# A state-space layer by chunks of four steps, with its matrices made during the feed-forward part ahead of it, and the pool half first

## The reference, cut to what matters

```
first block, for each of 2 layers:
    x = layer_norm(ALPHA*x + 0.5*swiglu(x, ffn1)); x = layer_norm(ALPHA*x + hybrid attention(x))
    x = layer_norm(ALPHA*x + 0.5*swiglu(x, ffn2))        # 1024 -> 2*2816 -> 1024
second block, layer 0:
    h = x @ ab_w_in                                      # 1024 -> 512 (state space) + 512 (pool)
    mix = concat(s5_mixer(h[:, :512]), pool_mixer(h[:, 512:])) @ ab_w_out
    x = layer_norm(ALPHA*x + mix)
    x = layer_norm(ALPHA*x + mixture of 16 experts(x) + gated projection of p)
layer 1: the same with stick-breaking attention as the mixer
```

## Time and profile before

| what | us |
|---|---|
| median of 3 runs | 1889.21 (1889.15 to 1889.84) |
| the profiled execution's own time | 1889.26 |
| its span | 1887.5 |
| last feed-forward part, about | 825 to 1009 |
| `s5_and_pool` on PE, about | 1009.5 to 1179.1 |
| PE busy over the span | 1787.5 (95%) |
| DVE, ACT, POOL busy | 953.6, 611.0, 149.4 |

### The profile page before, as it was taken

How to read it: one execution, slowest core, us unless ns; L and a number is a source line. 1 busy time by engine, 2 the same in 40 slices (tenths; PEclk the granted TensorE clock), 3 DMA queues, 4 the chain that set the end, 5 groups by cost and what they waited for, 6 DMA issues and landing times.

```text
span 1887.5 us, 24150 instructions
## 1 busy us (share of the span) xinstructions
PE 1787.5 (95%) x9722; PEld 1327.3 (70%) x9722; DVE 953.6 (51%) x1313; ACT 611.0 (32%) x750; POOL 149.4 (8%) x123
## 2 busy tenths in 40 slices
PE   6999999999999999999999678999998999999996
PEld 5888878788878888777887336855554777755553
DVE  3654767555555556768546994511113666511113
ACT  3543443443344335436434212210002344110110
POOL 1000051000000004110000340000000000000000
PEclk9999999999999999999999788999999999999998
DMA  7555532555455545064555002799998433799993
GB/s 274 186 179 198 195 118 90 200 188 191 178 201 184 194 178 201 24 239 179 190 188 185 21 0 89 286 422 421 421 422 322 162 134 123 313 421 421 422 422 127
DMA packets 59710, 420.43 MB, mean 223 GB/s; under 512 B 6737, under 2 KB 6737, under 8 KB 10225
## 3 DMA queue, kind: packets, MB, share of 16 engines
q1 hardware_dynamic: 55728, 404.78, 55.4%
q0 software_dynamic: 3904, 14.55, 2.3%
HBM read 418.25 MB, written 1.05 MB: 222 GB/s over the span
## 4 chain that ended last, share of the span: by engine, by line
PE 84%; DVE 9%; ACT 3%; issue 2%; POOL 1%; DMA 1%; DVEq 0%; POOLq 0%; ACTq 0%
PE hh L1089 12%; PE y L569 10%; PE y L571 10%; PE y L570 10%; PE hh L569 8%; PE hh L571 8%; PE hh L570 8%; PE turn L1115 6%; PE y L1128 3%; PE turn L1013 3%; ACT w_hi L1243 1%; DVE w_lo L1631 1%; DVE work L2054 1%; PE turn L685 1%; DVE work L2063 1%
## 5 line engine op out<-in xcount | busy, mean ns | idle before, releaser
L1631 DVE TENSOR_TENSOR w_lo<-raw,w_hi 128x2048 fp32r<-128x2048 f32 x181 | 410.9, 2289 | 159.2 <-ACT w_hi L1243 159.1
L1243 ACT ACTIVATE w_hi<-raw 128x2048 fp32r<-128x2048 f32 x193 | 364.6, 1912 | 64.9 <-DMA raw<-units 64.9
L569 PE MATMUL hh<-w_hi,xt_hi 128*128 128x512 f32 x704 | 279.8, 397 | 1.8 <-DVE xt_lo L1736 1.8
L571 PE MATMUL hh<-w_hi,xt_lo 128*128 128x512 f32 x704 | 275.3, 391 | 0.0
L570 PE MATMUL hh<-w_lo,xt_hi 128*128 128x512 f32 x704 | 275.2, 391 | 0.0
L569 PE MATMUL y<-w_hi,xt_hi 128*128 128x512 f32 (+1 forms) x480 | 191.7, 399 | 7.0 <-DVE xt_lo L2080 2.8
L571 PE MATMUL y<-w_hi,xt_lo 128*128 128x512 f32 (+1 forms) x480 | 186.9, 389 | 0.0
L570 PE MATMUL y<-w_lo,xt_hi 128*128 128x512 f32 (+1 forms) x480 | 186.9, 389 | 0.0
L569 PEld LDWEIGHTS hh<-w_hi,xt_hi 128*128 128x128 f32 x704 | 132.9, 189 | 30.1 <-DVE xt_lo L1736 2.9
L571 PEld LDWEIGHTS hh<-w_hi,xt_lo 128*128 128x128 f32 x704 | 132.7, 188 | 28.4
L570 PEld LDWEIGHTS hh<-w_lo,xt_hi 128*128 128x128 f32 x704 | 132.9, 189 | 26.3
(11 more groups left out here) (298 smaller groups left out, 2144.1 us busy)
## 6 DMA issues: line engine op xcount, KB each, us to landing
raw<-units SPq DMA_DIRECT2D x289, 1024.0 KB, 10.6
late<-units SPq DMA_DIRECT2D x96, 1024.0 KB, 11.3
ln_gb<-ln_g POOLq DMA_DIRECT2D x6, 512.0 KB, 4.0
ln_gb<-ln_b POOLq DMA_DIRECT2D x6, 512.0 KB, 5.6
x_rows<-x POOLq DMA_DIRECT2D x2, 512.0 KB, 10.0
work<-window_matrices POOLq DMA_DIRECT2D x1, 1024.0 KB, 11.0
ln_gb<-ln_mix_g POOLq DMA_DIRECT2D x2, 512.0 KB, 4.4
ln_gb<-ln_mix_b POOLq DMA_DIRECT2D x2, 512.0 KB, 5.3
```

What stands on the lines that cost most here:

```text
L569: pe.matmul(dst, left[0], right[0], start=start, stop=False)
L571: return pe.matmul(dst, left[1], right[0], start=False, stop=stop)
L1243: act.activation(hi[r][:, :], raw[r][:, :], ACT.Copy).then_inc(hi_ready, 1)
L1631: dve.tensor_tensor(lo[r][:, :], raw[r][:, :], hi[r][:, :].bitcast(F32), ALU.subtract)\
```

## The change

The recurrence is taken in chunks of four time steps. B' is multiplied by `lam^0` to `lam^3` (`in_weights`), so that one matmul of 64 columns (K = 4 steps x 32 inputs) gives what a chunk adds to the state; the scan runs over 64 chunks with `|lam|^4`; C is multiplied by `lam^1` to `lam^4` (`out_weights`), so that the state at a chunk's start gives four outputs; what the inputs of a chunk do to its own outputs goes through a 128x128 matrix for each distance 0 to 3 (`k_mat`). Four tiles of states are one scan of 256 columns, so there are 4 scans for each part, not 16. POOL has no part in it: DVE turns back as well.

The matrices, and the sines (now 128x1024 in all), are made during the last feed-forward part: DVE has seven asides instead of two, ACT three and then copies, PE three small pieces in each of four steps. For this the loop of that part is written out. The pool half of `x @ ab_w_in` comes first; the state-space half comes transposed from PE and is spread by ACT into `u_p` and `u_s` (one copy of 256 columns and 16 of 32x64 for each quarter). The window means use 144, 16 and 112 columns. Three quarters of the pool half's output product fill places between the `outputs`. `decay` lies where `h` and `gate_act` do. POOL clears two buffers with memsets, takes three small loads for five, and loads `p` only after the last scan.

```diff
--- before.py
+++ after.py
@@ POOL, last feed-forward part, and ahead of load_p(0)
+                    pool.memset(work[:, 3072:8192], 0.0).then_inc(zeros_made, 1)
+                    pool.memset(work[:, 10240:13312], 0.0).then_inc(zeros_made, 1)
...
+            pool.wait_ge(st_ready, 4)
             load_p(0)
-            for i in range(S5_TILES):
...
-                for j in range(2):
-                    pool.tensor_tensor(n5[b][:, j], s5[:, b], trig[i // 4 % 2][:, j, q:q + 1, :].broadcast_to([P, 2, T]),
@@ PE, feed-forward part: a step, written out up to step 9
                 def step(j):
+                    if beside is not None:
+                        beside(j, 0)
                     tile(h_bank, half=first_half)
+                    if beside is not None:
+                        beside(j, 1)
                     down(j == 1, False)
+                    if beside is not None:
+                        beside(j, 2)
                     turn_h()
@@ PE, s5_and_pool
+                def states(c):
+                    pe.wait_ge(u_ready, c + 1)
...
+                    for q in range(4):
+                        for ri in range(2):
+                            at = (4 * ri + q) * N_CHUNKS
+                            mm = pe.matmul(h_bank[c % 2][:, at:at + N_CHUNKS], w_in[:, c, ri, q, :], u_s[:, c, q, :],
+                                           start=True, stop=True)
+                def outputs(c):
+                    if c >= 2:
+                        pe.wait_ge(y_read, c - 1)
+                    dst = turn_bank[c % 2]
+                    for d in range(CHUNK):
+                        pe.matmul(dst[:, d * N_CHUNKS:T], k_mat[:, c, d, :],
...
+                    pe.wait_ge(st_ready, c + 1)
+                    for j in range(CHUNK):
+                        for ri in range(2):
+                            for q in range(4):
+                                mm = pe.matmul(dst[32 * q:32 * q + 32, j * N_CHUNKS + 1:(j + 1) * N_CHUNKS],
...
+                features(0)
+                features(1)
+                states(0)
+                features(2)
+                states(1)
+                features(3)
+                window_means()
+                states(2)
+                outputs(0)
+                pool_mix()
+                states(3)
+                outputs(1)
+                pe.wait_ge(xt_lo_ready, seen(xt_lo_ready))
+                pool_part(0, 0)
+                outputs(2)
+                pool_part(0, 1)
+                outputs(3)
+                pool_part(1, 0).then_inc(unit_used, 1)
+                pe.wait_ge(bu_read, 4)
                 w = unit(4)
...
+                gate(w, 0, 4)
+                pool_part(1, 1).then_inc(unit_used, 2)
+
                 pe.wait_ge(xt_lo_ready, seen(xt_lo_ready, 2))
...
+                four(y_bank[1][0][:, :], w[0], 0, 1, first=False, last=True).then_inc(unit_used, 1)
+                turn_x(0)
+                four(y_bank[1][1][:, :], w[1], 0, 1, first=False, last=True).then_inc(unit_used, 1)
@@ ACT, s5_and_pool
+                def features(m):
+                    act.wait_ge(u_done, m + 1)
...
+                    act.activation(u_p[:, m], src, ACT.Copy)
+                    for q in range(4):
+                        for k in range(CHUNK):
+                            ins = act.activation(u_s[32 * k:32 * k + 32, m, q, :], src[32 * q:32 * q + 32, CHUNK - 1 - k, :],
+                                                 ACT.Copy)
@@ DVE, asides of the last feed-forward part
+                return (s5_parameters, lambda: (s5_angles(), out_weights(1)), lambda: (out_weights(2), out_weights(3)),
+                        lambda: (out_weights(4), in_weights(0))) + tuple(lambda c=c: in_weights(c) for c in range(1, 4))
@@ DVE, s5_and_pool
+                    dve.tensor_tensor(m5[:, 0], bu, both(trig[:, 0]), ALU.mult).then_inc(dve_link, 1)
+                    dve.tensor_tensor(m5[:, 1], bu, both(trig[:, 1]), ALU.mult).then_inc(bu_read, 1)
...
+                    dve.tensor_tensor(m5[:, 0, 0], m5[:, 0, 0], m5[:, 1, 1], ALU.add).then_inc(dve_link, 1)
+                    dve.tensor_tensor(m5[:, 0, 1], m5[:, 0, 1], m5[:, 1, 0], ALU.subtract).then_inc(dve_link, 1)
...
+                        dve.tensor_tensor_scan(m5[:, 0, ri], wide(decay), m5[:, 0, ri], 0.0, ALU.mult, ALU.add)\
...
+                    link(dve.tensor_tensor(m5[:, 1], m5[:, 0], both(trig[:, 1]), ALU.mult))
+                    link(dve.tensor_tensor(m5[:, 0], m5[:, 0], both(trig[:, 0]), ALU.mult))
...
+                    dve.tensor_tensor(s[:, 0], m5[:, 0, 0], m5[:, 1, 1], ALU.subtract).then_inc(dve_link, 1)
+                    dve.tensor_tensor(s[:, 1], m5[:, 0, 1], m5[:, 1, 0], ALU.add).then_inc(st_ready, 1)
...
+                scan(0)
+                split_to(8)
+                scan(1)
...
+                ins.then_inc(xt_lo_ready, 1)
+                scan(2)
+                for part in range(4):
+                    gelu(0, part)
+                scan(3)
+                split_to(S5_UNITS)
+                for c in range(1, 4):
+                    for part in range(4):
+                        gelu(c, part)
```

More of the change, by code:

```diff
@@ L959, in s5_and_pool @@
-                mm.then_inc(pooled, 1)
-                def inputs(i):
-                    c, q = i // 4, i % 4
-                    if i >= 2:
-                        pe.wait_ge(scan_ready, seen(scan_ready))
-                    for ri in range(2):
-                        mm = pe.matmul(h_bank[i % 2][:, ri * T:(ri + 1) * T], bb_t[32 * q:32 * q + 32, ri, c, :],
-                                       ab_t[32 * q:32 * q + 32, c, :], start=True, stop=True)
-                    mm.then_inc(bu_ready, 1)
@@ new lines, in gate @@
+                def gate(w, first, last):
+                    for k in range(first, last):
+                        pe.wait_ge(xt_lo_ready, seen(xt_lo_ready))
+                        for m in range(4):
+                            mm = mm3(pe, h_bank[m // 2][:, (m % 2) * T:(m % 2 + 1) * T],
+                                     [v[:, k, m * P:(m + 1) * P] for v in w], (xt_hi[:, k, :], xt_lo[:, k, :]),
+                                     k == 0 and m % 2 == 0, k == 3 and m % 2 == 1)
+                            if k == 3 and m % 2 == 1:
+                                mm.then_inc(glu_done, 1)
@@ new lines, in s5_and_pool, with pool_part @@
+                w_out = []
+                def pool_part(t, c):
+                    if t == 0:
+                        w_out.append(unit(4))
+                    return four(y_bank[t][c][:, :], w_out[c], 1, t, first=True, last=False)
+                features(0)
[8 more added lines that the diff above has]
+                pool_mix()
@@ L1008, in gather @@
+                w = []
+                for c in range(2):
+                    w.append(unit(4))
+                    four(y_bank[0][c][:, :], w[c], 0, 0, first=False, last=True).then_inc(y_half, 1)
+                four(y_bank[1][0][:, :], w[0], 0, 1, first=False, last=True).then_inc(unit_used, 1)
+                turn_x(0)
+                four(y_bank[1][1][:, :], w[1], 0, 1, first=False, last=True).then_inc(unit_used, 1)
             def gather(l, p, half, dst):
@@ new lines, in times @@
+                def times(dst_re, dst_im, some, one_re, one_im, n_):
+                    one_re, one_im = (v.broadcast_to([P, n_, S5_TILES]) for v in (one_re, one_im))
+                    some_re, some_im = (v[:, some] for v in (lam_pow_re, lam_pow_im))
+                    product(dst_re, (some_re, one_re), (some_im, one_im), ALU.subtract, n_)
+                    product(dst_im, (some_re, one_im), (some_im, one_re), ALU.add, n_)
+                times(lam_pow_re[:, 1:2], lam_pow_im[:, 1:2], slice(0, 1), lam_pow_re[:, 0:1], lam_pow_im[:, 0:1], 1)
```

613 lines of the change are left out of this document (356 added, 257 removed).

## The result

The changed kernel takes 1833.95 us (median of 4 runs, 1830.02 to 1834.42) against 1889.19, a ratio of 0.970 (95% interval 0.9685 to 0.9719). Forecast were 1838.0, in a range of 1822 to 1860. The profiled execution took 1834.42, its span is 1832.7.

What follows compares the result with a forecast made beforehand. PE was taken to bound the feed-forward part, and a ring of DVE, POOL and PE the recurrence. The stage saves 71 us, 19.3 are added ahead: 51.7 off 1889.3 gives 1838, range 1822 to 1860.

Steps and rivals of the forecast that it cites:

- a ring with DVE nearly full: Old recurrence: PE waits by turns on POOL's turning back and DVE's scans; DVE busy 87 of 99.7 us.
- 1.0 us wait for unit 3: Start of the new stage: PE waits 1.0 us for unit 3, behind DVE's new `decay` copy of about 1.3 us.
- 7 off for the clock: New stage: lost clock at narrow stretches and waits (`outputs(0)`, pool product, gate, final products) costs 7 us, bounds 0 and 16.
- 0.3 us a copy: ACT's copies beside `features`: at 0.3 us each, 5 us a quarter, and PE would wait some 4 us in all.
- in different column groups run beside each other: Narrow matmuls overlap, clock holds: `outputs` 2 us, stage saves 80, PE's added pieces 8 instead of 12; 1825; chance 0.15.
- my other reading of that part: `outputs(0)`: weight loads overlap only matmuls of other row groups, so load and matmul add up to 0.08 us a record.
- The first rival: Narrow matmuls run at half clock: `outputs` 13 to 15 us, stage saves 60, time 1849; chance 0.2.
- pieces on PE: Four feed-forward steps: `k_mat` matmuls 1.7, transposes 0.9 and a wait of about 0.4 in each, 12 us in all.
- parameters' aside: Feed-forward part: 23 more small DVE operations ahead of a split PE already waits for; 4.0 us, counted in full.
- angles, step 2: Feed-forward part: ACT waits for angles, loads tables and makes sines, so the product comes about 1 us late.
- two `out_weights`, step 3: Feed-forward part: 16 DVE operations, 6.6 us, ahead of a split and the product, which comes 2.3 us late.
- The rivals on DVE and DMA: DVE's asides bound the feed-forward part: about 1893 or more, chance 0.03; experts' weights bound the end: few us gained, chance 0.02.

## Why the prediction was right, and where its terms were off

**The bound.** It held that the old stage was a ring with DVE nearly full, and that only this stretch and what is put into the full PE ahead of it matter. The 708.4 and 708.6 us behind the router show the first half, the 17.5 ahead of the stage the second.

**The stage: 71 saved, 72.5 measured.** Counted from the first `features`, as measured, and as forecast from the end of `first_tile` (with its 1.0 us wait for unit 3, which didn't come):

| point | forecast, full clock | measured |
|---|---|---|
| first k part of `outputs(0)` | 19.1 | 25.1 |
| end of the pool product | 27.1 | 29.2 |
| scan 2 starts | 30.5 | 32.7 |
| end of scan 3 | 47.0 | 48.1 |
| three gelus done | 60.6 | 59.8 |
| the last unit's output products start | 65.9 | 68.9 |
| `turn_x(0)` | 75.6 | 79.2 |
| router | 79.2 | 84.7 |

The forecast took 7 off for the clock and so had 86.2 at the router. The sum is right to 1.5 us, the terms are less so:

- Up to the first k part: 6 us dearer. ACT's sixteen copies were priced right at the upper end (3.59 us, 0.22 each), and 4.0 with the 256-column one, against PE's 2.9. That made the wait of 2.1 us, and the lower clock behind it cost 3.2 more. I had this wait only at 0.3 us a copy, and had put no loss of clock there. It was the dearest place of the changed kernel. The window means took 2.75 us where 1.5 stood, because I priced them by columns alone: two records of 16 columns take 0.13 us, six times what that price gives.

```profile
1060.30 0.29 PE L1027 MATMUL y<-masks,pool_rows 128*128 128x16 f32 x2
1060.43 0.46 PE L1028 MATMUL y<-masks,pool_rows 128*128 128x112 f32 x2
```

- Narrow records: 64 in 1.0 us where 5.1 stood. The rival "in different column groups run beside each other" was right in mechanism, and I gave it 0.15. Its prices were right too: 2 us for an `outputs` (2.3 measured) and 8 for PE's pieces (8.8, of which only 3.6 to 5.0 are matmuls and transposes). Its time of 1825 didn't come, since it also had the clock hold. The Trainium skill, in TensorE: Matmul & The Clock Gate, Part 3, has matmuls of other column tiles run at the same time; the rows agree (1.09 us in turn, 3.14 one group after the other), and my other reading of that part, that a load overlaps only matmuls of other row groups, doesn't hold here.
- Gelus: 3.1 us instead of 3.8, hand-overs being 0.48; the first 4.0 instead of 5.1. Together 3.1 less.
- The fourth k part, `outputs(3)`, waited until 1090.41 for the second gelu's first step. I had `outputs(3)` ending inside the gelus and the last quarter of the gate alone behind them; in fact a pool part and the whole gate (48 matmuls, 5.8 us, 1098.31 to 1104.07) stand behind it. From "gelus done" to the last unit's products it is therefore 9.1 us, where 5.3 stood. The order of PE in the changed kernel could have told, since each start follows from the one ahead.
- The last product at the lower clock, 4.4 for 2.7. In four of the eleven profiles with this product it kept the full clock, 2.9.

The clock's 7 us were a fair size but in other places than named: not in `outputs(0)` or in the narrow matmuls between dense ones, but behind waits of PE (2.1, 2.7, 5.0 and 1.8 us). Not every such wait cost clock: behind the one of 1.4 here, and behind the 1.9 in step 4, the clock held. That the sum came within 1.5 us is in part luck, as `features` and window means too dear and narrow records and gelus too cheap nearly cancel, and as the clock of one execution differs from that of the next by some us. The first rival (narrow matmuls drag the clock down) fell: 64 narrow records took 1.09 us at the full clock when dense work stood around them, and 1.91 at the lower one only behind waits of 2.7 and 5.0.

**The feed-forward part: 19.3 added, 17.5 measured.** By the steps:

| term | forecast | measured |
|---|---|---|
| pieces on PE | 12 | 8.8 |
| parameters' aside | 4.0 | 6.7 (4.4 of wait, 2.3 of clock behind it) |
| angles, step 2 | 1.0 | 0 |
| two `out_weights`, step 3 | 2.3 | 2.15 |

The aside was sized to the tenth in DVE's own time (4.2 for 4.0), and its "count in full" was right; what failed is that a wait costs more than its length where the clock falls behind it. The pieces were mis-sized in both directions: a `k_mat` record costs a quarter of its price, so that matmuls and transposes come to 3.6 (most of them left out) to 5.0 (doubled), and 1.0 of the rest of the 8.8 is waits, where I had 1.6. What the rest of it is stays open.

**The rivals on DVE and DMA** fell as expected. Broadcast inputs and outputs in runs of 16 cost nothing extra:

```profile
900.45 1.42 DVE L2155 TENSOR_TENSOR work<-work,params 128x256 f32<-128x256 f32 x4
901.91 0.42 DVE L2159 TENSOR_TENSOR work<-work 64x256 f32<-64x256 f32 x1
```

Four in 1.42 and single ones of 0.42 are the price of the earlier trace rows. POOL's memsets brought no wait.

## What to carry to other kernels

Where a small recurrence is bound by a vector engine and hand-overs, take several steps at once and move what doesn't depend on the data to an earlier stage in which that engine has slack; price what it adds there on the full engine, waits included. Count a wait of PE of some us as its length plus a loss of clock that differs by execution, here from nothing to 3.2 us, and fill it with other work of PE before anything else: here that gave 2.6 to 4.3 us in the profiles, and 5.8 in the median, for a wait of 2.1. Don't read the price of such an edit from one profile: put several beside each other and look where they part. Write down PE's whole order behind the last hand-over, not only the piece that the hand-over releases.

## What the runs showed of the hardware that was not expected

- Float32 matmuls with 32 weight columns that take turns over four column groups cost 0.014 us a record with 63 columns and 0.026 with 128; the same ones group by group cost 0.046 (63 columns). All of them use the full 128 rows.
- After the same wait of 3.1 us in one and the same kernel the clock fell in one execution and not in another (19.6 us against 16.9 to the next `turn_h`). Behind the longer wait of 5.67 us it fell in all seven profiles that have it, and cost 2.0 to 2.7 us.
- DVE beside POOL lost just what POOL took over: 4.63 us a tile alone, 4.5 with POOL.
